# Splitting the turned activations by token pairs behind a feed-forward, and weight rounding moved ahead of squares and head roots

## What is computed

```python
# end of the first block
ff = square(relu(h @ w_ff_in)) @ w_ff_out              # 512x1024 -> 4096 -> 1024
x  = layer_norm(ALPHA * x + (1 + g2) * ff, ln2_g, ln2_b)
# start of the second block
h  = x * rsqrt(mean(x*x) + 1e-6) * norm1_g
p  = h @ w_in_2        # 1024 x 2560: q, k, v (512 each), then conv and pool columns
q  = rms_norm_2(q, q_norm_g); k = rms_norm_2(k, k_norm_g)   # per head of 64
```

## Time and profile before

| | us |
|---|---|
| median of 3 runs | 1378.03 (1376.95 to 1379.72) |
| the profiled execution | 1377.24 |
| its span | 1375.5 |
| TensorE busy | 1324.8 (96% of the span) |
| VectorE busy | 836.8 (61%) |
| ScalarE busy | 657.6 (48%) |
| GpSimd busy | 623.4 (45%) |
| mean granted TensorE clock | 0.995 of full |

### The profile page before, as it was taken

The page is one execution under the profiler, slowest core; times in us unless marked ns, Lnnn a source line. Parts: engine busy times, 40 slices in busy tenths (PEclk is TensorE's granted clock), DMA queues, the critical chain, the costliest instruction groups (busy, mean ns, idle before and its releaser), DMA issues.

```text
span 1375.5 us, 16594 instructions
## 1 busy us (share of the span) xinstructions
PE 1324.8 (96%) x6471; PEld 1090.6 (79%) x6471; DVE 836.8 (61%) x1151; ACT 657.6 (48%) x919; POOL 623.4 (45%) x503
## 2 busy tenths in 40 slices
PE   2999999999999999999999996999999999999999
PEld 2888778888878888888888875887788888888887
DVE  6586987789861677708158396648722661906337
ACT  0645445466774165445353455424535544545353
POOL 0453855433335856251443505673744535153440
PEclk9999999999999999999999998999999999999999
DMA  9343534755324525867769543225133686766953
GB/s 341 114 109 124 118 123 147 207 157 172 116 64 154 165 82 127 219 161 151 229 126 254 129 104 122 92 92 128 52 99 124 142 225 150 165 203 153 244 122 92
DMA packets 149837, 202.93 MB, mean 148 GB/s; under 512 B 10140, under 2 KB 94384, under 8 KB 148480
## 3 DMA queue, kind: packets, MB, share of 16 engines
q1 hardware_dynamic: 123760, 146.95, 34.0%
q0 software_dynamic: 19760, 49.53, 17.7%
q10 hardware_dynamic: 6240, 5.40, 1.6%
HBM read 189.12 MB, written 2.26 MB: 139 GB/s over the span
## 4 chain that ended last, share of the span: by engine, by line
PE 87%; DVE 7%; POOL 2%; ACT 1%; issue 1%; DMA 1%; SPq 0%; ACTq 0%; DVEq 0%; POOLq 0%
PE bank L2098 26%; PE bank L2100 26%; PE bank L2099 26%; DVE tmp L1642 2%; PE bank L2304 2%; POOL w_lo L686 2%; PE bank L2314 1%; DMA arena<-in_w_ada_dram 1%; PE bank L2725 1%; PE bank L2497 1%; PE bank L2289 1%; PE bank L2317 1%; PE bank L2279 1%; PE bank L2498 1%; POOL w_lo L824 1%
## 5 line engine op out<-in xcount | busy, mean ns | idle before, releaser
L686 POOL TENSOR_TENSOR w_lo<-raw,w_hi 128x512 fp32r<-128x512 f32 x180 | 260.2, 1475 | 274.4 <-ACT w_hi L937 274.4
L2098 PE MATMUL bank<-w_hi,a_hi 128*128 128x512 f32 x864 | 341.3, 395 | 9.4 <-DVE a_lo L1433 6.2
L2100 PE MATMUL bank<-w_hi,a_lo 128*128 128x512 f32 x864 | 337.9, 391 | 0.0
L2099 PE MATMUL bank<-w_lo,a_hi 128*128 128x512 f32 x864 | 337.7, 391 | 0.0
L2098 PE MATMUL bank<-a_hi,w_hi 128*128 128x512 f32 (+1 forms) x832 | 321.4, 386 | 2.7 <-DVE a_lo L1433 1.7
L2100 PE MATMUL bank<-a_hi,w_lo 128*128 128x512 f32 (+1 forms) x832 | 317.5, 382 | 0.0
L2099 PE MATMUL bank<-a_lo,w_hi 128*128 128x512 f32 (+1 forms) x832 | 317.5, 382 | 0.0
L824 POOL TENSOR_TENSOR w_lo<-raw,w_hi 128x512 fp32r<-128x512 f32 x112 | 150.9, 1452 | 180.4 <-ACT w_hi L1060 180.4
L2098 PEld LDWEIGHTS bank<-w_hi,a_hi 128*128 128x128 f32 x864 | 163.1, 189 | 47.1 <-issue 10.2
L2100 PEld LDWEIGHTS bank<-w_hi,a_lo 128*128 128x128 f32 x864 | 162.9, 189 | 34.3
L2099 PEld LDWEIGHTS bank<-w_lo,a_hi 128*128 128x128 f32 x864 | 163.2, 189 | 32.6
(11 more groups left out here) (279 smaller groups left out, 1696.1 us busy)
## 6 DMA issues: line engine op xcount, KB each, us to landing
raw<-in_w_in_dram SPq DMA_DIRECT2D x24, 1024.0 KB, 5.2
raw<-in_w_mlp_dram SPq DMA_DIRECT2D x24, 1024.0 KB, 6.0
arena<-in_w_ada_dram SPq DMA_DIRECT2D x18, 1024.0 KB, 6.6
raw<-in_w_ff_in_dram SPq DMA_DIRECT2D x16, 1024.0 KB, 7.7
arena<-in_w_ff_out_dram POOLq DMA_DIRECT2D x13, 1024.0 KB, 8.7
arena<-in_w_mlp_dram POOLq DMA_DIRECT2D x13, 1024.0 KB, 8.6
raw<-in_w_out_dram SPq DMA_DIRECT2D x12, 1024.0 KB, 5.5
raw<-in_w_in_dram SPq DMA_DIRECT2D x16, 512.0 KB, 5.4
```

The lines of the kernel that those rows point to most:

```text
L686: last = pool.tensor_tensor(w_lo[:, u0 % 2, cols], raw[:, u0 % 2, cols], w_hi[:, u0 % 2, cols].bitcast(F32), ALU.subtract)
L2098: pe.matmul(out_, hi_a, hi_b, start=start, stop=False, skip_group_check=resumed)
L2099: pe.matmul(out_, hi_a, lo_b, start=False, stop=False, skip_group_check=resumed)
L2100: return pe.matmul(out_, lo_a, hi_b, start=False, stop=stop, skip_group_check=resumed)
```

## The change

**Order of the items.** `LN_ITEMS` gets a second list for the seam. Before, the items go k 0 to 3 of token pair 0, k 0 to 3 of pair 1, k 4 to 7 of pair 0, k 4 to 7 of pair 1. Now all eight k of pair 0 come first, then all of pair 1. The transposes of the other three groups follow items 1, 6 and 9 (before 2, 3 and 7), and unit +1 is needed from item 4 on.

**VectorE.** Gates and adds of the last quarter work on both token tiles of a block at once (128x2x512 in one instruction). M4's sum is read right behind M3's block, then the two shifts, and the remaining two blocks are finished between the first splits.

**ScalarE.** Only three halves are normalised ahead of the first item. Units +2 and +3 are both rounded behind the last item, unit +4 behind all four squares, ahead of the reads of group 0. In every quarter the roundings of two feed-forward operands stand ahead of the rounding of M5's weights.

**GpSimd.** The powers of the variances move by a piece; `both_parts(+1)` no longer waits for the first four splits, and the two row loads follow it. `rms_root` stands behind unit +4's remainder, and unit +5's remainder ahead of the first head root.

**SyncE and TensorE.** The first two loads of the projection are issued a unit earlier. `row_pair` waits for units +2 to +4 piece by piece.

```diff
-LN_ITEMS = [(pair, 4 * half + k) for half in range(2) for pair in range(2) for k in range(4)]
+LN_ITEMS = [[(pair, 4 * half + k) for half in range(2) for pair in range(2) for k in range(4)], [(pair, k) for pair in range(2) for k in range(8)]]
...
-            lo(U_QKV2, turn=1, root_at=1)
-            for t in range(2, TB):
-                ln_root(1, t)
+            lo(U_QKV2, turn=1)
+            both_parts(U_QKV2 + 1, (2, 3))
             load_row(1, ln2_g)
             load_row(2, ln2_b)
-            pool.wait_ge(a_lo_made, T_N2 + 4)
-            both_parts(U_QKV2 + 1)
             relative_tiles()
-            lo(U_QKV2 + 2)
+            lo(U_QKV2 + 2, parts=lo_part)
             relative_mask()
-            lo(U_QKV2 + 3)
+            lo(U_QKV2 + 3, parts=qkv_part)
+            lo(U_QKV2 + 4, parts=qkv_part)
             rms_root(2, EPS2)
-            lo(U_QKV2 + 4)
+            lo(U_QKV2 + 5)
             head_root(0, 0)
-            lo(U_QKV2 + 5)
             head_root(0, 1)
             lo(U_CP)
...
             for t in range(2):
-                normalize(1, t)
-            for js in (range(12), range(12, 16)):
+                normalize(1, t, (0,))
+            normalize(1, 0, (1,))
+            for js in (range(2), range(2, 16)):
                 affine_items(R_N2, T_N2, lambda k: mod[:, 64 + k:65 + k], lambda k: mod[:, 72 + k:73 + k], js)
                 if js[0] == 0:
-                    act.wait_ge(w_hi_made, U_QKV2 + 2)
-                    hi(U_QKV2 + 2)
+                    normalize(1, 1, (1,))
+            act.wait_ge(w_hi_made, U_QKV2 + 2)
+            hi(U_QKV2 + 2)
+            hi(U_QKV2 + 3)
...
-            squares(2, x1, junk, ln_made, lambda t: 4 + t + 1, U_QKV2 + 3)
+            squares(2, x1, junk, ln_made, lambda t: 4 + t + 1)
+            hi(U_QKV2 + 4)
             act.wait_ge(rs_made, 3)
             for n in range(3):
-                if n:
-                    hi(U_QKV2 + 2 * n + 2)
+                if n == 2:
+                    hi(U_QKV2 + 6)
...
+            def finish(step):
+
+                if step == 0:
+                    add_copied(READ_M2, OP_M2, 2)
+                    gate(READ_M2)
+                elif step == 1:
+                    add_block(READ_M2, 9)
+                else:
+                    add_copied(READ_M3, OP_M3, 4)
+                    gate(READ_M3)
+                    add_block(READ_M3, 10)
+                    read_product(U_FF1 + FF_OPS * (QUARTERS - 1), QUARTERS - 1, READ_M4, OP_M4, gate_product)
+                    shift(1, 0)
+                    shift(1, 1)
+                    gate(READ_M7)
+                    split_item(0, M_N2, lambda k: mod[:, 64 + k:65 + k])
+                    split_item(1, M_N2, lambda k: mod[:, 64 + k:65 + k])
+                    add_block(READ_M7, 11)
+                    split_item(2, M_N2, lambda k: mod[:, 64 + k:65 + k])
+                    split_item(3, M_N2, lambda k: mod[:, 64 + k:65 + k])
+                    dve.wait_ge(c_read, reads(QUARTERS - 1, READ_M4))
+                    add_block(READ_M4, 12)
...
-            row_pair(U_QKV2 + 2, 1, N_QKV2[1], 0)
-            row_pair(U_QKV2 + 4, 0, N_QKV2[0] + 1, 0)
+            row_pair(U_QKV2 + 2, 1, N_QKV2[1], 0, parts=((lo_part, 6), (qkv_part, 0)))
+            row_pair(U_QKV2 + 4, 0, N_QKV2[0] + 1, 0, parts=((qkv_part, 3), None))
```

More of the change, by code:

```diff
@@ L595, in _ @@
             feed_forward(U_FF1, 0, *ff_v[0], [(sum_made, 1)])
-            four_rows(U_QKV2, w_in2_v, 0, 0)
+            for b in range(2):
+                sp.wait_ge(w_lo_made, U_QKV2 + b - 2)
+                rows(0, 0, U_QKV2 + b, w_in2_v, 4 * b, 0, split=False)
+            for b in range(2, 4):
+                rows(0, 0, U_QKV2 + b, w_in2_v, 4 * (b % 2), 512)
             for b in range(2):
@@ L665, in both_parts @@
                 for part in range(4):
+                    if part == 2:
+                        for t in roots:
+                            ln_root(1, t)
                     cols = slice(512 * part, 512 * part + 512)
@@ L945, in turned_hi, with normalize @@
                     act.activation(a_hi[buf][:, k], bank[b][:], ACT.Identity, scale=scale, bias=bias).then_inc(a_hi_made, 1)
-            def normalize(turn, t):
+            def normalize(turn, t, halves=range(2)):
                 act.wait_ge(ln_shift, 2 * turn + t + 1)
-                for part in (slice(0, 512), slice(512, 1024)):
+                for half in halves:
+                    part = slice(512 * half, 512 * half + 512)
                     act.activation(x1[:, t, part], x1[:, t, part], ACT.Identity, scale=st[:, 8 + t:9 + t], bias=st2[:, 4 + t:5 + t]).then_inc(xhat_made, 1)
@@ L1972, in residual @@
                     dve.scalar_tensor_tensor(x1[:, t], x1[:, t], ALPHA, yacc[:, t], ALU.mult, ALU.add).then_inc(z_made, 1)
-            def gate_and_add(t, half, count, made):
-                part = slice(512 * half, 512 * half + 512)
-                if count is not None:
-                    dve.wait_ge(c_read, count)
-                    link(dve.tensor_tensor(yacc[:, t, part], yacc[:, t, part], row[:, 3, part], ALU.mult))
-                dve.tensor_tensor(x1[:, t, part], x1[:, t, part], yacc[:, t, part], ALU.add).then_inc(sum_made, 1)
-                dve.wait_ge(sum_made, made)
-                half_stats(t, half, 1 - t // 2)
@@ L1995, in last_product, with block_of, gate @@
-            def last_product(n, t, part, product, negative):
-                dve.tensor_tensor(yacc[:, t, part], product[:], row[:, 3, part], ALU.mult).then_inc(c_read, 1)
-                dve.wait_ge(c_read, reads(QUARTERS - 1, READ_M4, t - 2))
-                gate_and_add(t, 0, None, 13 + t)
+            def block_of(n):
+                pair, half = c_block(n)
+                return slice(2 * pair, 2 * pair + 2), slice(512 * half, 512 * half + 512)
+            def gate(n):
+                ts, part = block_of(n)
+                dve.wait_ge(c_read, reads(QUARTERS - 1, n))
+                block_ = yacc[:, ts, part]
+                link(dve.tensor_tensor(block_, block_, row[:, 3, part].unsqueeze(1).broadcast_to([P, 2, 512]), ALU.mult))
@@ new lines, in add_block, with add_copied @@
+            def add_block(n, made):
+                ts, part = block_of(n)
+                dve.tensor_tensor(x1[:, ts, part], x1[:, ts, part], yacc[:, ts, part], ALU.add).then_inc(sum_made, 1)
+                dve.wait_ge(sum_made, made)
+                for t in range(ts.start, ts.stop):
+                    half_stats(t, part.start // 512, 1 - t // 2)
+            def add_copied(n, op, copied):
+                u = U_FF1 + FF_OPS * (QUARTERS - 1)
+                dve.wait_ge(x_read, copied)
+                read_product(u, QUARTERS - 1, n, op, accumulate)
@@ L2166, in row_pair @@
                     wait = None if t0 is None else lambda kk: at(i, tstep, t0 + kk + 1)
[L2167 removed]
+                    row_half(u0, b, s, act_buf, 4 * b, b == 0, b == 1, wait, i, per, parts=parts and parts[b])
             def turn_pair(turn, pair, half):
```

144 lines of the change are left out of this document (74 added, 70 removed).

## The result

The changed kernel takes 1383.74 us (median of 7 runs, 1382.62 to 1385.74), the kernel before in the same sitting 1378.09 (1376.95 to 1379.72). The ratio is 1.0042, 95% interval 1.0033 to 1.0051: slower by 5.65 us. I had forecast 1378.9, with 1374.6 to 1381.9 as the range.

The account below looks back on a forecast made before the run. TensorE, busy for 1324.8 of 1375.5 us, was taken as the bound, its pause ahead of the items as VectorE's order of work. 1377.24 + 0.9 = 1378.1, and 0.8 more for the median: 1378.9; range 1374.6 to 1381.9.

Parts of the forecast that it names:

- the end of the sum: From VectorE's q scaling, forecast 2.9 us later, to the second head transposes: +0.9 us for the whole kernel.
- the margin of 2.05: Slack in us between q's last scaled piece (927.62) and TensorE's need in the second head transposes (929.7).
- group 0's reads against 886.5: ScalarE's four reads ahead of unit +4: their time against 886.5 was to give about the final shift in every rival.
- The front: Feed-forward's end through the items: first item at 831.9 (−7.2 us), item 4 at 842.2, items' end at 860.7 (−5.7).
- The two product waits: TensorE waits of 0.45 and 0.30 us in products before the items; removing them, with pipeline refill, was to give −1.2.
- rival 3: TensorE's half clock lasts after item 4, costing 2.6 us more by the items' end: +3.5, 1381.5; chance 0.09.
- Alternation: VectorE's gain operations and GpSimd's remainder pieces take turns: six at 2.46 us, last gain ending at 874.1.
- the steps given for item 4: VectorE's work from 828.1 through gate, adds, statistics and splits, said to bring item 4's split at 842.2.
- rival 2: GpSimd keeps the shared port for several pieces during gain: +3.5 to +4, 1381.5 to 1382; slower, chance 0.16.
- Rival 1: GpSimd's pieces and VectorE's gain hardly collide: −3.9, 1374.1 to 1374.9; chance 0.22.
- The back: Behind the items, from gain to group 0's reads: reads end at 887.4 instead of 879.9, unit +4 begins then.
- The wait in unit +3: TensorE's new wait for GpSimd's last remainder piece, which comes near 877.0: 3.3 us.

Follow-up runs that it names:

- the run without gain: Changed kernel with the second layer norm's gain and bias applied to only 16 of 1024 columns: 1381.20 us, against 1383.12 for the unchanged form beside it.
- copies later still: Kernel before, with eleven linked small copies on ScalarE ahead of the second pair of band copies: 1385.64 us against 1377.43, ratio 1.0053.

## Why the prediction was wrong

**The step that failed is the end of the sum.** I wrote "the margin of 2.05 takes all but 0.85 ... I take +0.9" and "In all of them the shift at the end is about that of group 0's reads against 886.5, since TensorE, VectorE and GpSimd hang on them". The chain was followed to q's scaling and to the first scores and left there. Behind it come ScalarE's copies of q and k, with 0.2 us to spare in the kernel before, and SyncE's load, whose issue hangs on other work. No rival had that mechanism: the three that I gave named a remainder, the port and the clock. The rows to read were there: in the trace before, the k pair is issued at 931.85 and lands 8.2 after the second's issue, at 940.6, and the second head's scores begin at 940.81. The sum moved the whole chain by 0.9 and never asked whether the load moves with it; it came 3.5 earlier and the copies 1.35.

**The front** was right: the first item at 831.0 for 831.9, item 4 at 840.7 for 842.2, the wait for the split of item 4 where I had put it. The two product waits went. The clock did not decide anything between the items (rival 3): it was back at 837.2.

**Alternation** was right in kind, and the price was some 9% high: 2.26 us from one gain operation to the next (860.70 to 871.98 in five steps), where I took 2.46, the sum of both alone. With the earlier start the last gain ends at 871.8 instead of 874.1. (As written, 857.1 + 2 × 1.2 + 6 × 2.46 is 874.3; the steps given for item 4 add up to 841.9 and those for unit +4's remainder to 883.3, where I had 842.2 and 883.6. None of it changes what follows.) The rule of the Trainium skill's page SBUF — State Buffer (section "SBUF: two separate sides"), that the loser waits for one instruction, holds in all six; rival 2, several pieces in a row, did not come up here. Rival 1, no collision, would have been worth some 1.9 us by the run without gain, not 4.8.

**The back** was too dear by 3 us. Unit +4's remainder had no VectorE work beside it and took 5.03, not 6.1; with the gain's 2.3 that is 3.4, the reads of group 0 ended at 884.0 and not 887.4. The wait in unit +3 was 1.1 and not 3.3. GpSimd's roots behind the remainders cost about 2 at the first scores (4.3 ahead of before with both undone, 2.15 with both as changed), for which I had charged 3.2 on the chain; and the base was 3 us earlier: VectorE scaled q at 914.3, 0.4 ahead of before instead of 2.9 behind.

So the seam came out 3 to 3.6 us better than I forecast, 2.15 to 2.7 ahead of before, and all of the loss lies in what I left out: 4.9 to 5.0 between the two heads' scores, where the copies meet the load, and 1.6 to 2.3 of half clock behind it. The two errors have opposite signs: 6.5 to 7.3 us were left out, and the better seam hides 3 to 3.6 of them.

## What to carry to other kernels

When a change moves one engine's chain and not another's, list the transfers of both that are in flight at the same time, and write down for each the time from its issue to its need. A transfer with 0.2 us of margin is a bound, even if no wait shows it. If a small urgent transfer and a large patient one can go out in either order, tie the large one behind the small one: the hold cost nothing in the kernel before (1.0002) and took back all of the loss in the changed one. And a sum ends at a place where all queues have met again, not at the first one that looks important.

## What the runs showed of the hardware

A pair of copies of 512 KB each from SBUF to SBUF was issued on ScalarE's queue behind such a pair, and a load of 1 MB on SyncE's. Where the load was issued 0.4 to 0.7 us before the last copy's issue was through, that copy took 10.7 to 13.0 us from the start of its issue to its landing (five traces); where it was issued 1.1 us or more behind that end, 7.8 to 8.5 (eight traces), the same as with the load over 6 us behind (7.9 to 8.4).

The packets say what lies between. The load's first data moved 3.0 to 3.5 us after its issue while copies were still in flight, and 1.0 to 1.2 after it with none. In the five slow traces 0.53 to 0.57 MB of the copies was left at that moment, in the others 0.13 or less. In one (copies later still) the load moved 0.75 MB in 3 us while the last copy moved nothing; in the other four both moved together. So the cost came where the last copy's data had yet to move when the load's began. No run separates the order of issue from that amount of overlap, and how the two queues are served no run here tells.

A wait of 4.7 to 5.5 us for that copy comes with TensorE's half clock in all five traces that have one, from 2.6 us before its end to 0.5 behind it on, and for 3.4 us in one and 6.8 in four; with waits of 0.8 and 0.9 it does not come. At 0.50 to 0.57 of its clock the engine is at the level of 1.2 GHz instead of 2.4. In some executions, of variants of the kernel before too, the clock is also at half between 188 and 195 us, which leaves the trace 2.1 to 2.4 us late against one without.
